# GpSimd divides the attention rows by their sums before the turn, and two output tiles begin inside the drain

## The reference

```
for l in range(2):
    h = rmsnorm(x, norm_g[l]);  proj = h @ w_in[l]            # (512,1024) @ (1024,4096)
    out_a = neighborhood_attention(q_a, k_a, v_a, na_rpb[l])   # 8 heads of 64
    out_b = diff_attention(q_b, k_b, v_b, t5_table, ...)       # 4 heads of 128
    y = concat([out_a * silu(g_a), out_b * silu(g_b)])
    x = x + y @ w_out[l]
return rmsnorm(x, final_g)
```

```
logits = einsum('bhcd,bhicjd->bhcij', qr, kr) * scale + bias
p = softmax(logits.reshape(b, h, 64, 8 * 16), axis=-1)
out = einsum('bhcij,bhicjd->bhcd', p, vr)
```

## Time and profile before

| | us |
|---|---|
| median of three runs | 941.54 |
| profiled execution, its time | 941.23 |
| profiled execution, its span | 939.4 |
| PE busy | 906.4 |
| PE weight load busy | 715.3 |
| DVE busy | 587.7 |
| ACT busy | 450.7 |
| POOL busy | 70.3 |

### The profile page before, as it was taken

The page is one execution under the profiler, slowest core; times in us unless marked ns, Lnnn a source line. Parts: engine busy times, 40 slices in busy tenths (PEclk is TensorE's granted clock), DMA queues, the critical chain, the costliest instruction groups (busy, mean ns, idle before and its releaser), DMA issues.

```text
span 939.4 us, 14917 instructions
## 1 busy us (share of the span) xinstructions
PE 906.4 (96%) x5861; PEld 715.3 (76%) x5861; DVE 587.7 (63%) x1200; ACT 450.7 (48%) x962; POOL 70.3 (7%) x89
## 2 busy tenths in 40 slices
PE   3999999999999999999999999999999999999996
PEld 1689888865667788887888877888887788887785
DVE  5899798998886472438862448344255965335733
ACT  4734223666784243436925348233434863436631
POOL 1001130006300010000010000000000010000002
PEclk9999999999999999999999999999999999999999
DMA  9735636266000232332304224122243222333203
GB/s 380 312 109 125 181 136 180 102 209 239 1 2 23 90 129 90 112 101 76 111 8 150 90 90 134 43 90 90 90 155 92 62 91 89 94 100 118 72 0 90
DMA packets 34647, 104.71 MB, mean 111 GB/s; under 512 B 14929, under 2 KB 14929, under 8 KB 32146
## 3 DMA queue, kind: packets, MB, share of 16 engines
q1 hardware_dynamic: 28098, 85.77, 27.5%
q0 software_dynamic: 3824, 15.73, 5.2%
q10 hardware_dynamic: 2656, 2.26, 1.0%
HBM read 98.37 MB, written 4.19 MB: 109 GB/s over the span
## 4 chain that ended last, share of the span: by engine, by line
PE 88%; DVE 6%; ACT 2%; issue 2%; DMA 1%; SPq 0%; POOL 0%; POOLq 0%; DVEq 0%; ACTq 0%
PE bank L1023 81%; PE bank L1384 2%; PE bank L1522 2%; DMA ring<-in_w_ada 1%; PE bank L1364 1%; DVE ring L2083 1%; PE bank L1440 1%; DVE arena L1651 0%; DVE ring L2282 0%; ACT ring L834 0%; PE bank L1430 0%; ACT arena L715 0%; DVE soft L2115 0%; ACT w_hi L882 0%; DVE soft L2093 0%
## 5 line engine op out<-in xcount | busy, mean ns | idle before, releaser
L2138 DVE TENSOR_TENSOR w_lo<-ring,w_hi 128x1024 fp32r<-128x1024 f32 x80 | 97.8, 1225 | 114.6 <-ACT w_hi L882 111.5
L1023 PE MATMUL bank<-w_hi,hT_hi 128*128 128x512 f32 x320 | 125.3, 392 | 1.3 <-issue 1.0
L1023 PE MATMUL bank<-hT_hi,w_hi 128*128 128x512 f32 x320 | 126.3, 395 | 0.0
L1023 PE MATMUL bank<-hT_lo,w_hi 128*128 128x512 f32 x320 | 124.6, 389 | 0.0
L1023 PE MATMUL bank<-hT_hi,w_lo 128*128 128x512 f32 x320 | 124.6, 389 | 0.0
L1023 PE MATMUL bank<-w_lo,hT_hi 128*128 128x512 f32 x320 | 124.6, 389 | 0.0
L1023 PE MATMUL bank<-w_hi,hT_lo 128*128 128x512 f32 x320 | 124.5, 389 | 0.0
L882 ACT ACTIVATE w_hi<-ring 128x1024 fp32r<-128x1024 f32 x80 | 84.4, 1058 | 11.6 <-PE bank L1023 11.4
L1023 PEld LDWEIGHTS bank<-w_hi,hT_hi 128*128 128x128 f32 x320 | 60.1, 188 | 14.7 <-issue 2.6
L1023 PEld LDWEIGHTS bank<-hT_hi,w_hi 128*128 128x128 f32 x320 | 60.1, 188 | 14.0 <-issue 0.7
L1023 PEld LDWEIGHTS bank<-hT_lo,w_hi 128*128 128x128 f32 x320 | 60.1, 188 | 12.8
(11 more groups left out here) (323 smaller groups left out, 1814.1 us busy)
## 6 DMA issues: line engine op xcount, KB each, us to landing
ring<-in_w_units SPq DMA_DIRECT2D x80, 512.0 KB, 3.6
ring<-in_w_ada SPq DMA_DIRECT2D x4, 2048.0 KB, 10.2
bias_ring<-in_na_bias POOLq DMA_DIRECT2D x8, 1024.0 KB, 5.5
ring<-in_w_out SPq DMA_DIRECT2D x2, 2048.0 KB, 8.7
bias_ring<-in_t_bias POOLq DMA_DIRECT2D x8, 448.0 KB, 3.8
x_t<-in_x SPq DMA_DIRECT2D x4, 512.0 KB, 5.9
arena<-in_w_ada SPq DMA_DIRECT2D x1, 2048.0 KB, 20.3
arena<-in_w_ada SPq DMA_DIRECT2D x2, 1024.0 KB, 23.2
```

Of the source, the lines that this page charges most:

```text
L1023: return pe.matmul(out, lhsT, rhs, start=first, stop=last)
L2138: dve.tensor_tensor(w_lo[:, u % 4], raw_w[:, u % 4], w_hi[:, u % 4].bitcast(fp32), SUB).then_inc(S["w_split"], 1)
```

## The change

GpSimd multiplies each half of a pair's rows by its inverse sum, in place, between `na_inverse` and `na_turn` (`na_scale`). PE's turn waits for that (`na_scaled`) in place of `na_exp`. The two identity products of each weighing and VectorE's product with the right half of the bank go. The lag between score and turn grows from 2 pairs to 3, on PE and ACT, and `na_out` stands two pairs later on DVE. The two half-layer waits for the last key tiles are spread over the first two steps. GpSimd's bias loads are issued between the scalings, one after every fourth pair. The first four steps of output tile 0 stand after weigh(12), those of tile 1 after weigh(15). In the first block the semaphore `kc_used` becomes a wait of VectorE for itself, and TensorE no longer waits for it.

```
+            def na_scale(l, m):
+
+                M = N_NA * l + m
+                pool.wait_ge(S["na_rinv"], M + 1)
+                for e in range(2):
+                    r = (2 * M + e) % 16
+                    p = prob2[:, m % 8, e * KW:(e + 1) * KW]
+                    pool.tensor_scalar(p, p, rinv[:, r:r + 1], None, MUL).then_inc(S["na_scaled"], 1)
...
-                for n in range(at_ + DAH + 2, min(at_ + LOADS + 2, LOADS * LAYERS)):
-                    load_bias(n)
+                for m in range(N_NA):
+                    na_scale(l, m)
+                    if m % NT == NT - 1 and at_ + DAH + 2 + m // NT < LOADS * LAYERS:
+                        load_bias(at_ + DAH + 2 + m // NT)
...
 (ACT)
-                        na_move(l, 0)
-                        for j in range(N_EARLY, N_NA + 2):
-                            na_move(l, j - 2)
+                        for j in range(N_EARLY, N_NA + NA_LAG):
+                            na_move(l, j - NA_LAG)
...
 (PE, na_turn and na_weigh)
-                    pe.wait_ge(S["na_exp"], 2 * M + e + 1)
+                    pe.wait_ge(S["na_scaled"], 2 * M + e + 1)
...
-                pe.wait_ge(S["na_rinv"], M + 1)
-                for e in range(2):
-                    hf = slice(e * HD, (e + 1) * HD)
-                    r = (2 * M + e) % 16
-                    ins = mm(out[hf, KW + m % 2 * P:KW + (m % 2 + 1) * P], rinv[:, r:r + 1].to_broadcast([P, HD]), ident, False, m % 2 == 1)
...
 (PE, the loop)
+                        for j in range(N_EARLY, N_NA + NA_LAG + 1):
                             if j < N_NA:
                                 na_score(l, j)
-                            if j == N_EARLY:
-                                pe.wait_ge(S["proj_evac"], pt2(l, 8) - 1)
-                                na_turn(l, 0)
-                                pe.wait_ge(S["proj_evac"], pt2(l, 8))
-                            if j < N_NA + 2:
-                                na_turn(l, j - 2)
-                            na_weigh(l, j - 3)
+                            if j <= N_EARLY + 1:
+                                pe.wait_ge(S["proj_evac"], pt2(l, 8) - 1 + j - N_EARLY)
+                            if j < N_NA + NA_LAG:
+                                na_turn(l, j - NA_LAG)
+                            if j > N_EARLY:
+                                na_weigh(l, j - NA_LAG - 1)
+                            if j == N_NA:
+                                out_rows(0, 6, range(0, 4))
+                        out_rows(1, 7, range(0, 4))
...
 (DVE)
-                tt(y, o[:, 256:512], y, MUL)
                 dve.tensor_tensor(y, o[:, 0:256], y, MUL).then_inc(S["na_out"], 1)
...
-                            if j >= 5 and j % 2:
-                                na_out(l, (j - 5) // 2)
+                            if j >= 7 and j % 2:
+                                na_out(l, (j - 7) // 2)
```

More of the change, by code:

```diff
@@ L400, in build @@
         MIX_LAG = 2
+        NA_LAG = 3
         GLU_BANKS = [7, 2, 3, 4]
@@ L1450, in tile_T, with tile_tok @@
                 return ins
-            def tile_tok(out, l, g, i, order=range(KD), between=None):
+            def tile_tok(out, l, g, i, order=range(KD), between=None, steps=range(KD)):
                 tok = slice(i * P, (i + 1) * P)
-                for m, k in enumerate(order):
+                for m in steps:
+                    k = order[m]
                     u = first_unit(l, g) + m // 2
@@ L1535, in na_weigh @@
                         hf = slice(e * HD, (e + 1) * HD)
-                        mm(out[hf, m % 2 * P:(m % 2 + 1) * P], src[:, b0 + b, (2 * p + e) * HD:(2 * p + e + 1) * HD],
-                           probT2[:, m % 4, e * KW + b * P:e * KW + (b + 1) * P], m % 2 == 0 and b == 0, False)
-                pe.wait_ge(S["na_rinv"], M + 1)
-                for e in range(2):
-                    hf = slice(e * HD, (e + 1) * HD)
-                    r = (2 * M + e) % 16
-                    ins = mm(out[hf, KW + m % 2 * P:KW + (m % 2 + 1) * P], rinv[:, r:r + 1].to_broadcast([P, HD]), ident, False, m % 2 == 1)
+                        ins = mm(out[hf, m % 2 * P:(m % 2 + 1) * P], src[:, b0 + b, (2 * p + e) * HD:(2 * p + e + 1) * HD],
+                                 probT2[:, m % 4, e * KW + b * P:e * KW + (b + 1) * P], m % 2 == 0 and b == 0, m % 2 == 1 and b == 1)
                 ins.then_inc(S["na_weighed"], 1)
@@ L1606, in _, with out_rows @@
                     else:
-                        for j in range(N_EARLY, N_NA + 3):
+                        def out_rows(t, b, steps):
+                            pe.wait_ge(S["na_taken"], 2 * (N_NA * (l + 1) - 1))
+                            pe.wait_ge(S["mixT_lo"], 4 * (l + 1))
+                            return tile_tok(bank[b], l, 8, t, OUT_ORDER, None, steps)
+                        for j in range(N_EARLY, N_NA + NA_LAG + 1):
                             if j < N_NA:
                                 na_score(l, j)
-                            if j == N_EARLY:
-                                pe.wait_ge(S["proj_evac"], pt2(l, 8) - 1)
-                                na_turn(l, 0)
-                                pe.wait_ge(S["proj_evac"], pt2(l, 8))
-                            if j < N_NA + 2:
-                                na_turn(l, j - 2)
-                            na_weigh(l, j - 3)
+                            if j <= N_EARLY + 1:
[7 more added lines that the diff above has]
+                        out_rows(1, 7, range(0, 4))
                 pe.wait_ge(S["na_taken"], 2 * N_NA * (l + 1))
-                pe.wait_ge(S["mixT_lo"], 4 * (l + 1))
-                def na_ready():
-                    pe.wait_ge(S["na_lo"], N_NA // 2 * (l + 1))
-                for t in range(8):
+                pe.wait_ge(S["na_lo"], N_NA // 2 * (l + 1))
+                for t in range(2):
+                    out_rows(t, 6 + t, range(4, KD)).then_inc(S["wo_done"], 1)
+                for t in range(2, 8):
                     c, i = divmod(t, 4)
-                    if t >= 2:
-                        pe.wait_ge(S["x_ready"], 8 * (l + 1) + t - 1)
+                    pe.wait_ge(S["x_ready"], 8 * (l + 1) + t - 1)
                     hook = None
-                    if t == 0:
-                        hook = na_ready
-                    elif t == 7 and l + 1 < LAYERS:
+                    if t == 7 and l + 1 < LAYERS:
                         hook = lambda: (rows_T(l + 1, 0), rows_T(l + 1, 1))
@@ L2342, in _ @@
                                 na_inverse(l, j - 1)
[L2343 to L2344 removed]
                             if j >= 7 and j % 2:
[L2346 to L2348 removed]
+                                na_out(l, (j - 7) // 2)
+                            if j >= 9 and j % 2:
+                                na_lo(l, (j - 9) // 2)
+                            if j >= 7 and j % 2:
+                                na_hi(l, (j - 7) // 2)
                             if j - MIX_LAG in MIX_AT:
@@ L2352, in _ @@
                         na_inverse(l, N_NA - 1)
-                        for g in range(N_NA // 2 - 2, N_NA // 2):
+                        for g in range(N_NA // 2 - 3, N_NA // 2):
                             na_out(l, g)
```

11 lines of the change are left out of this document (2 added, 9 removed).

## The result

The changed kernel takes 947.73 us (median of 4 runs, 946.51 to 948.23), against 941.65 (941.08 to 942.41, 4 runs) for the kernel before on the same chip: a ratio of 1.0062, 95% interval 1.0045 to 1.0079. It is 6.1 us slower. The forecast was 939.8 with a range of 936.2 to 945.0: the sign and the range were both wrong. The profiled execution took 948.23 (span 946.4, mean granted clock 0.995; before 939.4 and 0.996).

A forecast was written before the change was run, and what follows sets the result against it. TensorE, 88% of the chain, was taken as the bound. Removing 3.92 us a layer, less bias-load waits and a longer drain, left 0.88 a layer, 1.76 for two: 939.8 from 941.54, range 936.2 to 945.0.

The forecast's parts named there:

- the price of GpSimd's scaling: Each 128x256 multiply by a column on GpSimd: taken as 0.45 us, 1.0 us a pair with 0.05 between two.
- The far end: Upper price of one GpSimd scaling, 0.73 us, taken from its two-input operation of 2.37 us for 1024 columns.
- What is removed: Identity products taken from TensorE's weighings: 0.245 us a pair, 3.92 us a layer, leaving 1.70 us a pair.
- rival 1: Loop of loads is slack, TensorE alone limits: about 2.5 us gained a layer at best, 936.4 to 937.7; chance 0.24.
- The loop of loads: Bias loads, takes, reciprocals and scalings form one chain: turn 7 waits 0.6 us, turn 11 is 1.1 late.
- The core sign of the forecast: In the profile after, TensorE waits of 0.5 to 1.1 us ahead of turns 7 and 11.
- Mutual exclusion: GpSimd's scalings and VectorE's two-input operations lock each other out; without two mixT_lo stops, some 0.8 us more gain a layer.
- rival 2: GpSimd's scalings ahead of each turn become the bound at 2.21 us a pair: 946.9; chance 0.10.
- Output tiles begun early: Output products started in the drain: buy nothing of their own, as they had no wait to fill.
- point of decision: GpSimd scaling price at which its pair equals the earlier 1.94 us: 0.6 us an operation.
- Rival 3: First bias load's landing stays at 8 us, slowed by scalings and VectorE: 2.2 us lost a layer, 946.0; chance 0.12.

The follow-up runs named there:

- e4: Changed kernel with eight forms of GpSimd operation in place of the scaling, by pair, rows not rightly divided; a single run, 940.8 us, only durations count.
- e6: Changed kernel with the scaling as a two-input product and each bias load ahead of the scalings of pairs 3, 7, 11 and 15; 938.36 us.
- e7: Changed kernel with the scaling as a two-input product and the six bias loads of the stretch issued from SyncE's queue; 937.12 us.
- e1: Changed kernel without the scaling on GpSimd: rows left undivided, turns wait for the exponentials, GpSimd issues its bias loads alone; 937.37 us.
- e5: Changed kernel with only the scaling rewritten as a two-input product with the column broadcast, bias loads still behind the scalings; 941.32 us.
- e9: Changed kernel with its multiply by a column kept and the six bias loads moved to SyncE's queue; 942.10 us.
- e8: Changed kernel with the scaling moved to VectorE and the four mixT_lo products of a layer moved to GpSimd in exchange; 946.36 us.
- e11: Changed kernel with head 0 of each pair scaled by GpSimd and head 1 by VectorE, bias loads ahead of scalings 3, 7, 11 and 15; 941.16 us.
- e3: Kernel before with only the output tiles begun in the drain; lag, identity products and queues as before; 941.29 us.
- e2: Changed kernel with each bias load ahead of the scaling of pairs 3, 7, 11 and 15 instead of behind it; 944.96 us.
- e10: Changed kernel with both multiplies of each pair on VectorE, mixT_lo left there too, GpSimd issuing bias loads alone; 944.86 us.

## Why the prediction was wrong

The step that failed is the price of GpSimd's scaling: "I take 0.45, near the cast", with 0.73 as the far end. It is 0.92 alone and 0.986 on the mean. Both ends came from rows of other operations, and "Below the cast nothing speaks for it, as the multiply reads and writes as much" was a rule about bytes. What decides here is the operation: a copy and an addition over the same bytes take the 0.39 of the cast, the one-tensor multiply 0.84 and more (e4). The far end was no upper bound either, because it rested on the belief that two inputs are always dearer. With the cheap form and the loads out of the way the forecast's gain, and more, is there (e6, e7).

Point by point:
- *What is removed.* Right. TensorE's pair is 1.73 us in e1 (forecast 1.70), the second turn's wait went, score(5) waits 0.72 (0.7), and the gain with a free division is 3.7 us, or 2.35 a layer by the distances, where rival 1 had taken 2.5.
- *The loop of loads.* The mechanism exists, but not in this kernel. The landings, 5.6 and 5.3 us, were as taken (5.6 and 5.5); the bias waits of VectorE were 1.96 and 1.80, not about 1; the first load was issued 1.3 us later than forecast. Yet GpSimd has no gap, so they are the shadow of its backlog, not a cause, and TensorE waited at turns 4, 7, 8, 12 and 13: 0.2 us at turn 7, where 0.6 was forecast, and nothing at turn 11, where 1.1 was. The core sign of the forecast is missing. What the loads did cost in the changed kernel is GpSimd's own time, 0.6 to 0.8 us an issue in an unbroken chain. The sum never charged them, since it had GpSimd idle some 40% of the time (1.0 of 1.7 us a pair). From behind to SyncE, the loads are worth 5.0 us with the column multiply and 4.2 with the product, each against its own before (3.6 and 4.9 by the distances); only in e5 does part of the loop itself show (0.47 us at turn 7 of layer 1). In the changed kernel three issues stand in the chain in layer 0, 2.26 us, and two in layer 1, 1.62 (0.82 and 0.80 between starts). Layer 1 shows what the 3.6 are made of: there e9 has no bias wait at all and is 2.2 us shorter than the changed kernel (35.82 against 38.04), of which 1.6 are the two issues and 0.5 is a slightly faster pair (1.94 against 1.98). That leaves next to nothing for VectorE's late takes.
- *Mutual exclusion.* Shown (e8, e11, and mixT_lo in e5). "SBUF — State Buffer" of the Trainium skill, Who interferes with whom, adds that a multiply by a scalar on VectorE can take the shared ports too, and that who issues first holds them; both traces agree (0.62 to 1.54 where GpSimd was first, 0.92 to 1.20 where VectorE was). But its size in the changed kernel is small: 1.82 us a pair alone, 1.99 beside VectorE, so 0.17 a pair and not the 0.65 that rival 2 added. The forecast charged it to GpSimd alone; in e5 it was VectorE that was held, by 1.4 us.
- *Output tiles begun early.* Right: nothing of their own (e3).
- *Rivals.* Rival 2, GpSimd as the bound, is what happened, and its 946.9 is near 947.7, but by two errors that cancel: the operation dearer than its 0.73, the exclusion cheaper. With 0.92 put in, its own formula gives 2.59 us a pair, 0.65 too much over twenty pairs, 954.5. Its point of decision, 0.6 us an operation, seems to hold, as at 0.59 (e5) the kernel is level with before, but that is chance: GpSimd idles between scalings in e5, and e7, with the same operation, is 4.0 below before. I gave it 0.10, which was too little for an operation that no row showed, on an engine whose rows span from 0.8 to 2.1 ns a column. Rival 1's time (936.4 to 937.7) is that of e7, reached with another operation and another queue. Rival 3 did not occur in the changed kernel, though long landings came back in other runs: 7.6 us in both layers of e2, 8.8 in layer 1 of e6, 8.3 in layer 0 of e9.

## What to carry to other kernels

Before work goes to an engine that never did it in the trace, price that very operation (kind, form and width) and let the unknown widen the chances, not only the range; rows of other operations are no bounds. Then add up the receiving engine's whole queue between two fixed points, DMA issues included, and compare it with the pace of the engine that it feeds: here 11 x 1.95 + 2.26 us in layer 0, 23.7, against 19.0 for the same eleven pairs at TensorE's 1.73 told 4.7 of the 5.3 us that lie between the changed kernel and e1. If it doesn't fit, try the other forms of the same arithmetic, and move the issues to a queue that computes nothing, before giving the change up: these two edits turned 6.1 us lost into 4.0 gained.

## What the runs showed of the hardware

- GpSimd, 128x256 fp32 in SBUF, beside no locking work of VectorE (e4): copy 0.37 us, addition of a number 0.39, product of two tensors 0.59, multiply by a number 0.84, by a column 0.92. Dividing by broadcasting the column in a two-input product is a third cheaper than the multiply by a column.
- The same multiply on VectorE: 0.35 us for one, 0.62 for two (e8, e10).
- A bias load of 1 MB holds GpSimd 0.74 to 0.78 us to issue (rows L558 of the changed kernel) and its landing took 4.8 to 8.8 us over the kernels here. The first load of a layer, close to the last weight load, took 5.2 to 8.8 and the second 4.8 to 6.6.
- Two-input work and multiplies by a column on VectorE and the scalings on GpSimd hold each other up: mixT_lo, 0.67 us, took 2.05 when it began inside four scalings in a row (e5), and GpSimd's multiply took 1.20 instead of 0.92 when VectorE's had begun 0.06 us before it (e11).
